# Modulation columns from unsplit weights, the first norm applied to turned x, and the gate's weights summed on VectorE

## The reference

```python
mod = (jax.nn.silu(c) @ w_ada + b_ada)[:, None, :]      # 1024 x 3072 weights
shift, scale, gate = jnp.split(mod, 3, axis=-1)
h = rms_norm(x, norm_g) * (1.0 + scale) + shift
a_q, a_kv, ... = jnp.split(h @ w_in, IN_OFFSETS, axis=-1)
...                                                     # four attention branches, merged by gates computed from h
return x + gate * (merged @ w_out)
```

## Time and profile before

| | before |
|---|---|
| median of 3 runs | 1196.48 us (1195.12 to 1198.62) |
| profiled execution | 1198.76 us, its span 1197.5 us |
| mean granted TensorE clock | 0.984 |
| TensorE busy | 1158.2 us, 97% |
| VectorE busy | 736.3 us, 61% |
| ScalarE busy | 595.8 us, 50% |
| read from memory | 193.56 MB, 163 GB/s over the span |

### The profile page before, as it was taken

How to read it: one execution, slowest core, us unless ns; L and a number is a source line. 1 busy time by engine, 2 the same in 40 slices (tenths; PEclk the granted TensorE clock), 3 DMA queues, 4 the chain that set the end, 5 groups by cost and what they waited for, 6 DMA issues and landing times.

```text
span 1197.5 us, 16726 instructions
## 1 busy us (share of the span) xinstructions
PE 1158.2 (97%) x7018; PEld 1028.1 (86%) x7018; DVE 736.3 (61%) x938; ACT 595.8 (50%) x824; POOL 48.3 (4%) x80
## 2 busy tenths in 40 slices
PE   6999999999998998999999999999899999999997
PEld 4799888788888987898999998787787989999986
DVE  5944766566677997654566555455667556556543
ACT  5545754344454672554635444445565455444432
POOL 3020100000000000000100000000003000000000
PEclk9999999899999998999999999999899999999999
DMA  9884543265545502543654654655235535555450
GB/s 346 301 243 117 183 148 117 88 228 184 203 146 193 177 1 71 176 141 106 181 177 144 208 182 170 211 176 176 72 105 189 176 114 171 178 176 191 145 192 36
DMA packets 105932, 195.70 MB, mean 163 GB/s; under 512 B 6033, under 2 KB 22561, under 8 KB 105856
## 3 DMA queue, kind: packets, MB, share of 16 engines
q1 hardware_dynamic: 102976, 186.46, 46.8%
q0 software_dynamic: 2880, 8.17, 2.5%
HBM read 193.56 MB, written 1.05 MB: 163 GB/s over the span
## 4 chain that ended last, share of the span: by engine, by line
PE 77%; DVE 12%; ACT 6%; issue 2%; DMA 2%; POOL 1%; SPq 0%; DVEq 0%; ACTq 0%; POOLq 0%
PE product L541 69%; DVE conv_out L2322 4%; DVE w_low L497 3%; ACT w_high L488 2%; DMA w_raw<-in_w_ada 1%; PE small L659 1%; PE small L1795 1%; PE small L1178 1%; ACT drows L2673 1%; PE small L1189 1%; PE small L574 1%; DVE drows L2749 1%; DVE stats L2751 1%; PE small L1816 1%; DVE drows L2764 0%
## 5 line engine op out<-in xcount | busy, mean ns | idle before, releaser
L497 DVE TENSOR_TENSOR w_low<-w_raw,w_high 128x2048 fp32r<-128x2048 f32 (+3 forms) x184 | 404.4, 2203 | 269.0 <-ACT w_high L488 265.2
L488 ACT ACTIVATE w_high<-w_raw 128x2048 fp32r<-128x2048 f32 (+3 forms) x184 | 337.9, 1841 | 185.1 <-PE product L541 161.9
L541 PE MATMUL product<-H_low,w_high 128*128 128x256 f32 x1080 | 308.4, 286 | 5.2 <-DVE w_low L497 4.2
L541 PE MATMUL product<-H_high,w_low 128*128 128x256 f32 x1080 | 306.5, 284 | 0.0
L541 PE MATMUL product<-H_high,w_high 128*128 128x256 f32 x1080 | 306.1, 283 | 0.0
L541 PEld LDWEIGHTS product<-H_low,w_high 128*128 128x128 f32 x1080 | 207.8, 192 | 7.6 <-DVE w_low L497 4.5
L541 PEld LDWEIGHTS product<-H_high,w_low 128*128 128x128 f32 x1080 | 207.9, 193 | 0.3
L541 PEld LDWEIGHTS product<-H_high,w_high 128*128 128x128 f32 x1080 | 207.8, 192 | 0.0
L541 PE MATMUL product<-w_high,H_low 128*128 128x512 f32 (+2 forms) x384 | 151.4, 394 | 0.0
L541 PE MATMUL product<-w_low,H_high 128*128 128x512 f32 (+2 forms) x384 | 149.6, 389 | 0.0
L541 PE MATMUL product<-w_high,H_high 128*128 128x512 f32 (+2 forms) x384 | 149.3, 389 | 0.0
(11 more groups left out here) (371 smaller groups left out, 1532.3 us busy)
## 6 DMA issues: line engine op xcount, KB each, us to landing
w_raw<-in_ffn_w_gate SPq DMA_DIRECT2D x20, 1024.0 KB, 5.1
w_raw<-in_ffn_w_up SPq DMA_DIRECT2D x20, 1024.0 KB, 5.3
w_raw<-in_ffn_w_down SPq DMA_DIRECT2D x20, 1024.0 KB, 5.0
w_raw<-in_w_merge SPq DMA_DIRECT2D x16, 1024.0 KB, 5.0
w_raw<-in_w_ada SPq DMA_DIRECT2D x12, 1024.0 KB, 7.0
w_raw<-in_w_in SPq DMA_DIRECT2D x8, 1024.0 KB, 5.5
w_raw<-in_mem_w_k SPq DMA_DIRECT2D x8, 1024.0 KB, 5.0
w_raw<-in_conv_w_pw SPq DMA_DIRECT2D x16, 512.0 KB, 4.5
```

The lines of the kernel that those rows point to most:

```text
L488: k.act.eng.activation(chunk_view(k, k.w_high[j], i), chunk_view(k, k.w_raw[i % k.N_RAW], i), ACT.Copy).then_inc(*k.act.tells("weights_hig ...
L497: k.vec.eng.tensor_tensor(low, raw, high.bitcast(F32), ALU.subtract).then_inc(*k.vec.tells("weights_low", ("weights low", i)))
L541: mm = pe.eng.matmul(bank[:, off:off + wide], a, r, start=b not in started, stop=True, skip_group_check=True)
```

## The change

Five things change together.

1. Scale and shift are computed as columns. `pe_modulation` takes a chunk of w_ada as loaded, each 128x128 block of it as the stationary operand, and multiplies it with one column of silu(c). That is 16 products a chunk with one column each, float32 on both sides, summed in one bank for each half of the features. Nothing of these eight chunks is split. `k.split` lists the chunks that still are.
2. The first norm works by feature. ScalarE scales x by the root of its rows (`scaled_x`), TensorE transposes that (`pe_turn_x`), and VectorE applies gain and shift as two numbers of each partition (`vec_first_half`); then both engines split it.
3. norm_g and the biases of scale and shift are loaded as rows of 128 and turned with one transpose. x comes through SyncE's queue, between the fourth and the fifth chunk.
4. The gate's four chunks stand later in the plan, one behind each block of w_in from "c_qk" to "b_vz". VectorE multiplies each of their rows with its number of silu(c) and sums (`vec_gate_sums`), four instructions a chunk behind the split of the chunk ahead. The bias lies in the first partition of the sum at the start.
5. The sum over the partitions is two products with ones in `mem`, and VectorE scales them by a quarter there.

The last chunk of shift and the first two of w_in are interleaved in the plan: shift, w_in, shift, w_in.

```diff
+def modulation(ada, name, n):
+
+    at = ("shift", "scale", "gate").index(name) * D + n * CN
+    return [(pieces, nk, (name, n, f)) for f, (pieces, nk, _) in zip(range(0, KT, CK), chunks(ada, KT, [(at, CN)]))]
...
-    add(ada, *[[(c, CN)] for c in (D, 0, D + CN, CN, 2 * D, 2 * D + CN)])
-    add(w_in, [(W_D_Q, 512)], [(W_D_V, 512)], [(W_C_Q, 512)], [(W_C_V, 512)])
-    add(w_in, [(W_B_Q, 384)], [(W_B_V, 384)])
+    first_in, shift = chunks(w_in, KT, [(W_D_Q, 512)]), modulation(ada, "shift", 1)
+    plan.extend(modulation(ada, "scale", 0) + modulation(ada, "shift", 0) + modulation(ada, "scale", 1) + [shift[0], first_in[0], shift[1], first_in[1]])
+    add(w_in, [(W_D_V, 512)])
+    gate = modulation(ada, "gate", 0) + modulation(ada, "gate", 1)
+    for block in ((W_C_Q, 512), (W_C_V, 512), (W_B_Q, 384), (W_B_V, 384)):
+        add(w_in, [block])
+        plan.append(gate.pop(0))
...
+        if i + 1 < len(k.plan) and k.plan[i + 1][2] and k.plan[i + 1][2][0] == "gate":
+            vec_gate_sums(k, *k.plan[i + 1][2])
+
+
+def vec_gate_sums(k, name, n, first):
+
+    V, i = k.vec, k.whole_weights[name, n, first]
+    raw, total = chunk_view(k, k.w_raw[i % k.N_RAW], i), k.gate[:, n * CN:(n + 1) * CN]
+    V.wait_ge("c silu", ("weights", i), "gate bias")
+    for j in range(CK):
+        V.wait_ge(V.last)
+        V.eng.scalar_tensor_tensor(total, raw[:, j, :], k.c_silu[:, first + j:first + j + 1], total, ALU.mult, ALU.add).then_inc(
+            *V.tells("gate_sums", ("gate", n), ("weights low", i)))
...
 def pool_condition(k):
     w, g = k.w, k.pool
-    g.wait_ge("common")
-    g.eng.dma_start(k.b_ada[:, :], w["b_ada"][0:1, :]).then_inc(*k.landed("load_b_ada", "b_ada"))
-    pool_row(k, "load_norm_g", k.norm_g[:, :], w["norm_g"][0], "norm_g")
-    g.eng.dma_start(k.X[:, :, :], w["x"][0].rearrange("(t p) n -> p t n", p=P)).then_inc(*k.landed("load_x", "x loaded"))
+    for name, vector in (("norm_g", w["norm_g"][0]), ("shift", w["b_ada"][0, 0:D]), ("scale", w["b_ada"][0, D:2 * D])):
+        g.eng.dma_start(k.cond_rows[ROWS[name]:ROWS[name] + KT, :], vector.rearrange("(k p) -> k p", p=P)).then_inc(*k.landed("load_rows", "condition rows"))
+    g.eng.memset(k.gate[:, :], 0.0).then_inc(*g.tells("pool_steps"))
+    g.wait_ge(g.last)
+    g.eng.dma_start(k.gate[0:1, :], w["b_ada"][0:1, 2 * D:3 * D]).then_inc(*k.landed("load_gate_bias", "gate bias"))
+    pool_inverse_root(k, "first", k.stat(("sums", "first"), NT), D, RMS_EPS, "first squares")
     at = 0
     for source, row, n in VECTORS.values():
         vector = w[source] if row is None else w[source][row]
         g.eng.dma_start(k.vector_rows[at:at + n, :], vector.rearrange("(k p) -> k p", p=P)).then_inc(*k.landed("load_vectors", "vectors"))
         at += n
-    pool_inverse_root(k, "first", k.stat(("sums", "first"), NT), D, RMS_EPS, "first squares")
     g.ended("condition")
...
+def pe_modulation(k, name, n, first):
+
+    pe, i, key = k.pe, k.whole_weights[name, n, first], ("columns", n)
+    bank, at = k.product.take(key), CK * ("scale", "shift").index(name)
+    begins = (name, first) == ("scale", 0)
+    raw = chunk_view(k, k.w_raw[i % k.N_RAW], i)
+    pe.wait_ge("c silu", ("weights", i), k.product.before(key) if begins else None)
+    for j in range(CK):
+        for c in range(CK):
+            mm = pe.eng.matmul(bank[:, at + c:at + c + 1], raw[:, j, c * P:(c + 1) * P], k.c_silu[:, first + j:first + j + 1],
+                               start=begins and j == 0 and c == 0, stop=True, skip_group_check=True)
+    mm.then_inc(*pe.tells("columns", key, ("weights low", i)))
+
+
+def pe_turn_x(k, n):
+    for b in range(2):
+        bank = k.small.take(("x", n, b))
+        k.pe.wait_ge("scaled x", k.small.before(("x", n, b)))
+        for j in range(2):
+            for t in range(NT):
+                c = (CK * n + 2 * b + j) * P
+                tr = k.pe.eng.transpose(bank[:, j * S + t * P:j * S + (t + 1) * P], k.scaled_x[:, t, c:c + P], k.ident)
+        tr.then_inc(*k.pe.tells("turned", ("x turned", n, b)))
+
+
 def pe_condition(k):
-    pe = k.pe
+    pe, tr = k.pe, k.pe.eng.transpose
     pe.wait_ge("common", "c row")
...
+    tr(k.small.take("c")[:, 0:KT], k.c_row[:, :], k.ident[0:KT, 0:KT]).then_inc(*pe.tells("turned", "c turned"))
+    for name in ("scale", "shift"):
+        for first in range(0, KT, CK):
+            pe_modulation(k, name, 0, first)
+    pe.wait_ge("condition rows")
+    tr(k.small.take("condition")[:, 0:3 * KT], k.cond_rows[:, :], k.ident[0:3 * KT, 0:3 * KT]).then_inc(*pe.tells("turned", "condition turned"))
+    pe_modulation(k, "scale", 1, 0)
+    pe_turn_x(k, 0)
+    pe_modulation(k, "scale", 1, CK)
+    pe_modulation(k, "shift", 1, 0)
+    pe_turn_x(k, 1)
+    pe_modulation(k, "shift", 1, CK)
     pe.ended("condition")
+
+
+def act_first_half(k, n):
+    A = k.act
+    for b in range(2):
+        at = slice(CK * n + 2 * b, CK * n + 2 * b + 2)
+        A.wait_ge(("whole", n, b))
+        A.eng.activation(k.H_first.high[:, at, :], k.whole[:, 2 * b:2 * b + 2, :], ACT.Copy).then_inc(*A.tells("operand_high", ("first high", n, b)))
 
 
...
 def act_condition(k):
     A = k.act
     A.wait_ge("c turned")
-    A.eng.activation(k.c_silu[:, :], k.small.of("c")[:, 0:KT], ACT.Silu).then_inc(*A.tells("c_silu", "c silu", k.small.free("c")))
+    A.eng.activation(k.c_silu, k.small.of("c")[:, 0:KT], ACT.Silu).then_inc(*A.tells("c_silu", "c silu", k.small.free("c")))
+    sums = k.stat(("sums", "first"), NT)
+    for t in range(NT):
+        A.wait_ge("x loaded")
+        A.eng.activation(k.scaled_x[:, t, :], k.X[:, t, :], ACT.Square, accum_out=sums[:, t:t + 1]).then_inc(*A.tells("squares", "first squares"))
+    for t in range(NT):
+        A.wait_ge(A.last, ("root", "first"))
+        A.eng.activation(k.scaled_x[:, t, :], k.X[:, t, :], ACT.Copy, scale=k.stat(("root", "first"), NT)[:, t:t + 1]).then_inc(*A.tells("scaled_x", "scaled x"))
+    act_first_half(k, 0)
     act_split(k, 0)
+    act_first_half(k, 1)
     act_split(k, 1)
...
     A.ended("condition")
...
+def vec_first_half(k, n):
+    V, columns, ps = k.vec, k.stat(("columns", n), 2 * CK), k.product.of(("columns", n))
+    at = slice(CK * n, CK * (n + 1))
+    gain, bias, scale = (k.cond_cols[:, ROWS[name]:ROWS[name] + KT][:, at] for name in ("norm_g", "shift", "scale"))
+    V.wait_ge(V.last, ("columns", n))
+    V.eng.tensor_tensor(columns[:, 0:CK], ps[:, 0:CK], scale, ALU.add).then_inc(*V.tells("vec_steps"))
+    V.eng.tensor_tensor(columns[:, CK:2 * CK], ps[:, CK:2 * CK], bias, ALU.add).then_inc(*V.tells("vec_steps", k.product.free(("columns", n))))
+    V.wait_ge(V.last)
+    V.eng.scalar_tensor_tensor(columns[:, 0:CK], columns[:, 0:CK], 1.0, gain, ALU.add, ALU.mult).then_inc(*V.tells("vec_steps"))
+    for b in range(2):
+        for j in range(2):
+            f = 2 * b + j
+            V.wait_ge(V.last, ("x turned", n, b))
+            V.eng.tensor_scalar(k.whole[:, f, :], k.small.of(("x", n, b))[:, S * j:S * (j + 1)], columns[:, f:f + 1], columns[:, CK + f:CK + f + 1],
+                                ALU.mult, ALU.add).then_inc(*V.tells("whole", ("whole", n, b), k.small.free(("x", n, b))))
+    for b in range(2):
+        at = slice(CK * n + 2 * b, CK * n + 2 * b + 2)
+        V.wait_ge(("first high", n, b))
+        V.eng.tensor_tensor(k.H_first.low[:, at, :], k.whole[:, 2 * b:2 * b + 2, :], k.H_first.high[:, at, :].bitcast(F32), ALU.subtract).then_inc(
+            *V.tells("operand_low", k.H_first.ready(n)))
+
+
 def vec_condition(k):
     V = k.vec
...
+    V.wait_ge("condition turned")
+    V.eng.tensor_copy(k.cond_cols[:, :], k.small.of("condition")[:, 0:3 * KT]).then_inc(*V.tells("cond_cols", k.small.free("condition")))
+    vec_first_half(k, 0)
     vec_split(k, 0)
+    vec_first_half(k, 1)
     vec_split(k, 1)
...
     V.ended("condition")
...
     def mem():
+        for n in range(D // CN):
+            bank = k.small.take(("gate sums", n))
+            k.pe.wait_ge(("gate", n), k.small.before(("gate sums", n)))
+            k.pe.eng.matmul(bank[:, :], k.ones, k.gate[:, n * CN:(n + 1) * CN], start=True, stop=True).then_inc(*k.pe.tells("spread", ("gate sums", n)))
+        yield
...
+        for n in range(D // CN):
+            V.wait_ge(("gate sums", n))
+            V.eng.tensor_scalar(k.gate[:, n * CN:(n + 1) * CN], k.small.of(("gate sums", n))[:, :], 0.25, None, ALU.mult).then_inc(
+                *V.tells("gate", "layer gate", k.small.free(("gate sums", n))))
+        yield
...
+        if into == ("scale", 1, 0):
+            sp.eng.dma_start(k.X[:, :, :], w["x"][0].rearrange("(t p) n -> p t n", p=P)).then_inc(*k.landed("load_x", "x loaded"))
```

101 lines of the change are left out of this document (23 added, 78 removed).

## The result

| | before | changed |
|---|---|---|
| median | 1197.51 us (1195.12 to 1198.62, 4 runs) | 1212.51 us (1212.08 to 1216.14, 4 runs) |
| profiled execution, span | 1198.76, 1197.5 us | 1212.42, 1211.1 us |
| mean granted clock | 0.984 | 0.984 |

The ratio is 1.0131, 95% interval 1.011 to 1.0151. Forecast were 1211 us and a range of 1203 to 1218. Every difference in this study is under 2%, so each is read from its interval, and one whose interval does not contain 1 is taken as shown.

The account below looks back on a forecast made before the run. TensorE, busy 97% of the span, was taken as the bound. First w_in block +10.5, gate's sums +2.1 and sums across partitions +2.0 gave +14.6 us, on the median 1196.5 making 1211; range 1203 to 1218 us.

Parts of the forecast that it names:

- The start: Condition stage's beginning: first chunk of w_ada landed, so the single-column products can start, at 6.9 us.
- The pace: Single-column products of scale and shift on TensorE: slow clock throughout, 0.215 us for each of 256 instructions, 55.0 us.
- The stage: Whole condition stage on TensorE: the first w_in product can start at 65.8 us, against 57.5 before.
- The block behind it: First block of w_in, 96 products: first 48 begin at the slow clock; block ends at 79.5 us against 69.0, +10.5.
- Just in time: First w_in block: norm's second half and second weight split end at 73.1 us, first 48 products at 73.8; no wait.
- The gate's sums: VectorE's four groups of sums: only the fourth makes TensorE wait, +2.1 us, with 0 and 3.2 as ends.
- The sums over the partitions: Two f32 products 128x512 on TensorE in mem(), at the fast clock: +2.0 us, ends 1.7 and 2.1.
- The sum of +14.6: Whole kernel: 10.5 for the first w_in block, 2.1 for the gate, 2.0 for the sums across partitions.
- A: Condition stage: fast clock during the narrow products, first w_in product at 39.6 us, total 1184 us; chance 0.09.
- B: Condition stage: clock rises half way, behind the transposes say, 13.6 us less, total 1197 us; chance 0.05.
- C: VectorE's gate sums: all lie on the path, 12.6 us instead of 2.1, total 1221 us; chance 0.06.
- D: Behind the condition stage: the shift is swallowed later; no size given, no chance of its own.

## Why the prediction was right

**The start.** Forecast 6.9 us, measured 7.74. I had taken the first chunk to land earlier than the 7.13 of before, and it landed later; in the experiments with modulation columns TensorE began between 7.5 and 9.6.

**The pace.** The step on which all else hung was 0.215 us an instruction because narrow products keep the slow clock. Measured 0.213. That it is the clock, and the clock the columns, is shown by two pairs of runs: 128 columns for one brought 0.112, and one and the same row of 64-column products went at 0.213 or at 0.111, by what had stood ahead of it. The Trainium skill's columns / 1.2 ns for a load ("TensorE: Matmul & The Clock Gate", "LDWEIGHTS (loading the stationary operand)"), an estimate of 107 ns for 128 columns, agrees with the 0.11 us of the fast clock; wherever the pace was the slow one, it was the double.

**The stage.** Forecast first product 65.8, measured 65.86: 0.84 more at the start, and the 256 instructions 54.4 instead of 55.0 (58.12 us less 1.74 twice and 0.23), the rest a little under.

**The block behind it.** The rise of the clock at 69.85 instead of 70.8 put the first 48 products' end at 73.5 (73.8 forecast), and the norm's second half with the split ended at 73.66 (73.1). "Just in time" was so: the 49th product starts 0.2 us later than the pace would have it (0.34 us after the 48th, where 0.12 is the pace). +10.5, as forecast.

**The gate's sums.** Mis-sized: +2.1 forecast, +4.8 measured. VectorE's times were right (L1214 at 137.94, and the last of the four steps, L982, ends at 140.41; the forecast, moved by the 10.5, says 137.9 and 140.5). I took the wait to show at retention's result, the last of the four steps, and most of it showed at the first of them, where stick-breaking's product waits. That alone changes no sum: in the kernel with 128 columns the two waits together cost the 2.1 us forecast. The step that failed is that a wait was priced with its own length only. What it cost in clock, 2.7 us, I left out, although the prediction had just rested on narrow products losing the clock. Taking the wait away gave 4.9 us back.

**The sums over the partitions.** +2.0 forecast; the row says 1.88, the distance between the traces grows by 1.76.

**What made up for it.** 10.45 + 4.8 + 1.8 is 17.05, the spans differ by 13.6. By the distance between like instructions of VectorE, 1.65 us come back between 243 and 254 us of the kernel before and 1.8 more after 309, there around the stretch at 460 to 467 us where the clock falls in both, in the changed one for less long. The first place in windows of the kernel before, then of the changed one 15 us later:

```profile
242.00:244.00 2.00, 2.00 (x6) 1.54 (x5) 1.22 (x3) 0.67 (x3) 0.00 (x0) 0.50 1.04 408
244.00:246.00 2.00, 2.00 (x7) 1.58 (x6) 0.00 (x0) 2.00 (x7) 0.00 (x0) 0.67 1.04 375
```

```profile
254.00:258.00 4.00, 4.00 (x25) 3.27 (x24) 2.64 (x7) 0.00 (x0) 1.81 (x3) 1.00 0.81 270
258.00:262.00 4.00, 4.00 (x20) 3.29 (x19) 0.50 (x2) 3.43 (x9) 0.00 (x0) 1.00 1.01 360
```

Nothing of the change touches these places; what moved the clock there is not shown. The sum of +14.6 was thus near for two reasons. One is its main term, which was understood. The other is luck: two errors of about 3 us, the gate's and this one, cancelled. The second I saw no way to forecast from the trace of before, and it belongs in the width of a range.

**The rivals.** A fell by the pace; it is the kernel with 64 columns behind 128, 1185 us. B (a rise half way) did not happen with single columns, but with 64 it does, at just the place it named, the transposes. C fell: only one group of the sums is on the path. D (the shift is swallowed later), which had been given no chance of its own, came in part: some 3.4 of the 17.05 us.

## What to carry to other kernels

Before products with few columns replace wide ones, read the pace of the nearest narrow row at both clocks, and take the slow one for a long row of them: here the change took some 20 us of work each from VectorE and ScalarE, neither of which was the bound, and put 17 on TensorE, which was. Where a weight load sets the pace anyway, copies of a column up to 128 cost nothing that these traces show (0.213 us with 1, 64 or 128 columns at the slow clock, 0.112 with 128 and 0.111 with 64 at the fast one) and can be what brings and holds the clock. A wait of 1 to 3 us should be priced with a possible fall of the clock as well as with its own length: the fall came behind six of the seven waits of 2.53 us here, and behind two of the five of 1.75 to 1.92.

## What was not expected of the hardware

- One and the same row of 64-column products went 0.21 us apart from 8 to 42 us when it stood first, and 0.111 apart when 128-column ones had gone before.
- At 64 columns a wait of 0.99 us was followed by a fall of the clock (0.57 on the mean of 8 us), while 128 columns went through one of 0.78, in one profile each.
- A 128-column f32 instruction takes 0.112 us in a row, not the quarter of 0.525 that a 512-column one suggests.
- In all these profiles the clock column reads 1.00 from the start of the kernel to the first fall, also over 58 us at half the pace.
- The same wait of 2.53 us at the same place was followed by a fall in six profiles of seven, and for between 3 and 7 us; without one it cost 2.1 us, with one 4.8.
